# Twelve gate scatters and two gate loads moved across a block boundary in a decoder-layer kernel

## The reference, cut to what matters

```python
q = (tb @ wq).reshape(PEER_BLOCK, PEER_HEADS, 2, PEER_QHALF)
sc = jnp.einsum('thpd,hpnd->thpn', q, keys)
s1, i1 = lax.top_k(sc[:, :, 0], 16); s2, i2 = lax.top_k(sc[:, :, 1], 16)
# the best 16 of the 256 sums are the experts eidx, their softmax the gates g
act = jax.nn.gelu(jnp.einsum('td,thkd->thk', tb, u_tab[eidx]))
out = jnp.einsum('thk,thkd->td', g * act, v_tab[eidx])
```

## Time and profile before

| | us |
|---|---|
| median of three runs | 3581.18 (3580.72 to 3588.79) |
| the profiled execution | 3575.43 |
| its span, first to last instruction | 3573.7 |
| TensorE matmul busy | 3357.5 (94%) |
| VectorE busy | 2622.8 (73%) |
| GpSimd busy | 2051.8 (57%) |

### The profile page before, as it was taken

One profiled execution on the slowest core, in us unless ns is written; L12 is line 12 of the kernel. 1 busy time (PEld: TensorE's weight loads), 2 busy tenths in 40 slices (PEclk: granted clock), 3 DMA queues, 4 the chain that ended last, 5 costly groups with the idle time before them and its releaser, 6 DMA issues.

```text
span 3573.7 us, 41306 instructions
## 1 busy us (share of the span) xinstructions
PE 3357.5 (94%) x12551; PEld 1744.3 (49%) x12551; DVE 2622.8 (73%) x5429; ACT 842.2 (24%) x1786; POOL 2051.8 (57%) x1620
## 2 busy tenths in 40 slices
PE   8999799799899977799999999999999999999898
PEld 5676464444444445444444444444444444444343
DVE  3444584467778766578887888888888888888884
ACT  2333560344443465111111111111111111111021
POOL 0000100078888888577777777777777677777540
PEclk9999899899999988899999999999999999999999
DMA  4000631588889885899999999999999999999961
GB/s 148 30 29 15 243 146 68 179 213 213 205 211 233 226 229 147 263 396 407 405 407 398 400 406 404 403 394 406 406 406 404 396 391 407 405 401 398 355 218 42
DMA packets 410615, 1023.34 MB, mean 286 GB/s; under 512 B 93965, under 2 KB 130030, under 8 KB 406834
## 3 DMA queue, kind: packets, MB, share of 16 engines
q0 software_dynamic: 221184, 604.27, 46.6%
q1 hardware_dynamic: 175138, 394.69, 31.5%
q10 hardware_dynamic: 14096, 22.02, 1.7%
HBM read 972.05 MB, written 48.77 MB: 286 GB/s over the span
## 4 chain that ended last, share of the span: by engine, by line
POOL 21%; DMA 19%; issue 9%; DVE 7%; PE 2%; ACT 0%; DVEq 0%; SPq 0%; ACTq 0%; POOLq 0%
DMA u<-in_peer_u,idx_all 19%; POOL v L2165 11%; POOL u L2157 10%; DVE u L2175 2%; DVE facc L2203 2%; PE e_b L2319 1%; PE e_b L2090 1%; DVE wq L2203 1%; DMA w_room<-x_scratch 1%; DVE k_room L2105 1%; PE e_b L2307 0%; DVE ln_st L1060 0%; DVE w_room L2389 0%; DVE w_room L1073 0%; DVE w_room L2360 0%
## 5 line engine op out<-in xcount | busy, mean ns | idle before, releaser
L2157 POOL DMA_INDIRECT u<-in_peer_u,idx_all x576 | 724.8, 1258 | 393.2 <-DVE act L2175 246.4
L2090 PE MATMUL e_b<-w_room,e_room 128*128 128x512 f32 x2048 | 908.1, 597 | 21.7 <-DVE k_room L2105 12.8
L2175 DVE CUSTOM_DVE_ANT_0 u<-u,xb 128x1024 f32<-128x1024 f32 x576 | 705.7, 1225 | 295.1 <-DMA u<-in_peer_u,idx_all 268.5
L2058 PE MATMUL e_b<-wq 128*128 128x512 f32 x2048 | 900.3, 592 | 0.0
L2165 POOL DMA_INDIRECT v<-in_peer_v,idx_all x576 | 690.5, 1199 | 214.1 <-issue 177.5
L1782 POOL DMA_INDIRECT gate_scratch<-e_room,slot_of x384 | 610.4, 1590 | 188.3 <-issue 120.9
L2090 PEld LDWEIGHTS e_b<-w_room,e_room 128*128 128x128 f32 x2048 | 390.9, 191 | 519.4 <-issue 491.8
L2058 PEld LDWEIGHTS e_b<-wq 128*128 128x128 f32 x2048 | 379.5, 190 | 429.0 <-issue 429.0
L2203 DVE SCALAR_TENSOR_TENSOR facc<-v,w,facc 128x1024 f32<-128x1024 f32 x317 | 406.5, 1282 | 1.4
L2203 DVE SCALAR_TENSOR_TENSOR wq<-v,w,wq 128x1024 f32<-128x1024 f32 x254 | 325.9, 1283 | 0.5
L2051 ACT ACTIVATE wq<-e_b 128x512 f32<-128x512 f32 x256 | 140.0, 594 | 722.3 <-PE e_b L2044 473.2
(11 more groups left out here) (387 smaller groups left out, 3543.4 us busy)
## 6 DMA issues: line engine op xcount, KB each, us to landing
wq<-in_peer_u SPq DMA_DIRECT2D x128, 512.0 KB
w_room<-in_peer_v SPq DMA_DIRECT2D x128, 512.0 KB, 22.6
w_room<-in_cache_v SPq DMA_DIRECT2D x144, 256.0 KB
w_room<-in_cache_k SPq DMA_DIRECT2D x128, 256.0 KB
gate_scratch<-zeros SPq DMA_DIRECT2D x24, 1024.0 KB, 27.0
wq<-gate_scratch SPq DMA_DIRECT2D x96, 256.0 KB
u<-in_cache_k SPq DMA_DIRECT2D x64, 256.0 KB
xb<-in_cache_k SPq DMA_DIRECT2D x64, 256.0 KB
```

Of the source, the lines that this page charges most:

```text
L2058: last = pe.matmul(AQ[c % 2][:, 0:DT], UT[c % 2][:, k, :], x1Td[:, k, :], start=(k == 0), stop=(k == KC - 1))
L2090: last = pe.matmul(OQ[i % 2][b][:], WT[n % 2][:, c, m * P:m * P + P], Vd[(4 * n + c) % NVD][:, b * 512:b * 512 + 512], start=(c == 0), sto ...
L2157: pool.indirect_dma_start(u[x % NU], None, a["peer_u"], bass.IndirectOffsetOnAxis(ap=idx_all[:, t, h, j:j + 1], axis=0)).then_inc(s_u[x % ...
L2175: dve.tensor_tensor_reduce(u[x % NU], u[x % NU], xb[t % 2][:], 1.0, 0.0, ALU.mult, ALU.add, act16[k % 2][:, j:j + 1]).then_inc(s["ufree"], 1)
```

## The change

`scatter_pool` of the last head h = 7 issues ranks j = 0 to 11 only. Its last four ranks (`LATE_J = 4`), 4 x 3 = 12 scatters, are issued in the dense block by GpSimd: two behind each of the first six gather positions. `load_g(0)` leaves the end of the first block. In the dense block SP issues `load_g(0)` and `load_g(1)` behind `slot_sp(2)`, that is behind `load_u(5)`; the call for group 1 at x = 1 is gone.

```diff
-    LAG, WEIGH = 7, 5
+    LAG, WEIGH, LATE_J = 7, 5, 4
...
-        def scatter_pool(pool, h):
+        def scatter_pool(pool, h, js):
...
-            for j in range(TOPK):
+            for j in js:
                 for m in range(NSC):
                     if j == 0:
                         wait(pool, s_gs[m], 16 * TOPK * h)
-                    pool.indirect_dma_start(gate_d[m].rearrange("e (t o) -> (e t) o", o=1),
-                                            bass.IndirectOffsetOnAxis(ap=slot_of[:, m, h, j:j + 1], axis=0),
-                                            gd[:, m, h, j:j + 1], None, compute_op=ALU.add).then_inc(s_gs[m], 16)
+                    scatter_one(pool, h, j, m)
+
+        def scatter_one(pool, h, j, m):
+            pool.indirect_dma_start(gate_d[m].rearrange("e (t o) -> (e t) o", o=1),
+                                    bass.IndirectOffsetOnAxis(ap=slot_of[:, m, h, j:j + 1], axis=0),
+                                    gd[:, m, h, j:j + 1], None, compute_op=ALU.add).then_inc(s_gs[m], 16)
...
-            if x % 4 == 1 and x // 4 + 1 < NGR:
+            if x % 4 == 1 and 1 < x // 4 + 1 < NGR:
                 load_g(sp, x // 4 + 1)
...
                 load_x(sp, 1)
-                load_g(sp, 0)
...
-                    scatter_pool(pool, h)
+                    scatter_pool(pool, h, range(TOPK - (LATE_J if h == PH - 1 else 0)))
...
                     slot_sp(sp, x)
+                    if x == 2:
+                        load_g(sp, 0)
+                        load_g(sp, 1)
...
+                late = [(j, m) for j in range(TOPK - LATE_J, TOPK) for m in range(NSC)]
                 for x in range(NPOS + 12 + LAG):
                     gather_pool(pool, x)
+                    for j, m in late[2 * x:2 * x + 2]:
+                        scatter_one(pool, PH - 1, j, m)
```

## The result

The changed kernel takes 3592.53 us (median of 20 runs, 3582.47 to 3598.01), the kernel before in the same runs 3580.55 (3575.47 to 3590.75): ratio 1.0032, 95% interval 1.0024 to 1.0039. That is 12.0 us slower by the medians, where 11.4 was forecast (3592.6). The profiled execution took 3587.21 us, its span is 3585.4, against 3575.43 and 3573.7.

The account below looks back on a forecast made before the run. The barrier, then VectorE up to weigh(0, 0), then TensorE were taken to bound the kernel. VectorE 21.25 us later in the block, less 9.84 gained, gave +11.41 on the 3581.18 median: 3592.6 us, range 3584 to 3601.

Parts of the forecast that it names:

- The gain at the barrier: Barrier ahead of the dense block: without the last 12 scatters and `load_g(0)` the block starts 9.84 us earlier.
- T: The dense block's start, forecast at 1451.46: SP's last issue over at 1449.39, plus 2.07; 1461.30 before.
- GpSimd's string: Dense block: six gathers and 12 late scatters on GpSimd, the last scatter ready 31.5 us in (30.2 to 38.4).
- The landing of a scatter: Dense block: from the last late scatter being ready to SP going on, 5.45 us (2.4 to 6.3).
- rival A: Late scatters in the dense block land faster; at 2.4 us the net is +8.4, 3589.5 us; chance 0.23.
- The landing of the gate load: Dense block: the last of group 0's four 256 KB gate loads lands in 3.9 us, upper bound 10.3.
- Does it reach TensorE: From gating chunk 0 to weigh(0, 0): VectorE's delay reaches TensorE, weigh(0, 0) starts at 1527.6, 11.4 us later.
- rival C of the experiments: Ahead of the dense block: the changed programs are by themselves a few us slower there; no chance given.
- C: Gating of chunk 0: the wait stays hidden and the 9.84 us gain stands, 3571.3 us; chance 0.04.
- D: Barrier: something else holds it and the block starts no earlier, +21.3, 3602.4 us; chance 0.03.
- Rival E: Dense block: VectorE's 1.70 us and later idle times shrink, giving part back; net +8 to +9.5; chance 0.07.
- B: Crowded dense-block stretch: scatters at 2.22 or a gate load at 10.3, about +18, 3599 us; chance 0.11.

Follow-up runs that it names:

- second profile of before: Kernel before, unchanged, profiled once more, with TensorE's last scores group ahead of the barrier starting at 1455.54; ratio 1.0000 (0.9990 to 1.0009).

## Why the prediction was right in its sum, and where it wasn't in its terms

**What bounds the kernel.** Right. From weigh(0, 0) to the end both kernels need the same, 2057.5 and 2056.8.

**The gain at the barrier: mis-sized.** Forecast T = 1451.46, measured 1454.06 and 1459.90. The 9.84 us were read from one execution, in which TensorE was early and stood for 12.91 us. The profiles of before show that this idle time is a cover: TensorE's path ahead of it varies by 8 us, and the block's start by 1. The step of the argument that failed is "TensorE's own work ends at 1448.39", taken as a fixed date. At a like E the gain is 11.4 in an early execution (E to T 14.0 against 2.6) and about 4 in a late one (6.8 against 2.9). The 2.07 from SP's last issue to the block's start was carried over wrongly as well: where SP's issue holds the barrier it is 0.45, in the changed kernel (1453.61 to 1454.06) and in the late profiles of before. A sign was there: the profiled execution lay 5.75 below the median of the runs, which the prediction added back without asking what it was.

**GpSimd's string.** 31.5 forecast, 33.4 and 32.5 in the two profiles of the changed kernel (1487.42 - 1454.06; 1492.37 - 1459.90). Single scatters took 2.10 and 2.29, in the second profile 2.59, where the others took 1.54 to 1.57, and single gathers up to 1.92 where most took 0.99. By the Trainium skill (SBUF — State Buffer, section SBUF: two separate sides) the prediction had estimated that hold-ups beside five dot products could come to 6 us; the traces show 2 to 3.

**The landing of a scatter: mis-sized.** 5.45 forecast, 1.5 (1487.42 to 1488.91) and 1.7 measured for the last scatter: rival A, and even below its bound of 2.4. Both rows that the 5.45 was argued from stood in crowded stretches. The prediction held against A that the 6.29 was measured at a share of 0.63, but this is the mean of 123 us; in the 6.3 us of the landing itself the share was 1.08 (first line; the second is the landing ahead of the barrier, the third the one in the changed kernel; the last three numbers are clock, DMA share, GB/s):

```profile
1351.80:1358.10 6.30, 1.63 (x2) 0.35 (x3) 4.10 (x21) 0.00 (x0) 3.10 (x3) 0.56 1.08 342
1453.40:1458.90 5.50, 0.00 (x0) 0.00 (x0) 0.00 (x0) 0.00 (x0) 0.05 (x1) 0.50 1.11 380
1487.40:1488.90 1.50, 1.30 (x4) 0.23 (x2) 0.00 (x0) 0.00 (x0) 1.02 (x2) 1.00 0.26 0
```

So the reading that was held against A was a mean over the wrong stretch. The rule of the Trainium skill (DMA: Bandwidth & Descriptors, section Anatomy of one DMA), about 2 us for a transfer so small, was nearer than my row for this landing; at a share of 1.1 both landings took over twice as long as the rule says.

**The landing of the gate load.** 3.9 forecast, 4.4 (1488.91 to 1493.28) and 4.6 measured. The 2.6 that the prediction worked out for it goes by a rule that it gives itself as one for GpSimd's transfers; this load is SP's.

**The gating of chunk 0.** T + 40.85 forecast, T + 39.22 and T + 38.72 measured: 1.6 to 2.1 too late, since the scatter's landing outweighs the other two.

**Does it reach TensorE.** Right at every step. Gating 0 to weigh(0, 0) took 35.30 and 35.45, forecast 35.30. TensorE's stall ahead of it was 12.58, between the 5.4 and 16 that were named; meet 5 was over at T + 61.9, ahead of the latest date of T + 70.7. Weigh(0, 0) took 9.88 instead of 8.91, about 1 more, within the bounds of 0 and 1.9; but the second profile of before has 10.02 behind a stall of 6.72, so this isn't the change's.

**The sum.** In the first pair of profiles the net is 1528.58 - 1516.20 = 12.4 us at weigh(0, 0) and 11.7 at the end. That this is near the forecast is chance: 4.2 of the 12.4 is E, which happened to be later. At a like E the profiles say (the changed kernel's 77.1 is taken to hold at any E, as it does in its two profiles, at 1451.5 and 1457.0):

| | gain at the barrier | cost behind it | net |
|---|---|---|---|
| forecast | 9.84 | 21.25 | 11.4 |
| early (first profiles) | 11.4 | 19.6 | 8.2 |
| late (second profiles) | 3.9 | 17.8 | 13.9 |

For an execution like the one it was read from, the forecast set the gain 1.6 too low and the cost 1.6 too high, and the net came out 3.2 too high. For a late one it set the gain 6 and the cost 3.5 too high. The timed 12.0 (8.6 to 14.0) lies between the two nets, and so does the forecast: its closeness is luck.

The late case is the usual one by an estimate. The median of before in the same runs, 3580.55, less the 1.7 around the span and the 2056.2 to 2057.8 that its profiles have from weigh(0, 0) to the end, puts weigh(0, 0) at 1521.0 to 1522.6, where its three profiles have 1516.2 to 1518.7; with the 63.2 to 63.6 of the late profiles E is at 1457 to 1459. The same for the changed kernel (3592.53, 2056.7 and 77.1) gives 1457. By this estimate E is no later in the changed program, which speaks against rival C of the experiments, and the net to expect is nearer 13.9 than 8.2. It also fits that moving only the loads gained nothing: in late profiles E to weigh(0, 0) is 63.2 without that move and 63.2 with it. The estimate takes it that the end part is as long in the executions that weren't profiled; in the fourteen that were it is 2055.2 to 2059.4.

**The rivals.** Rivals C and D are out: the wait at the gating is there, and E to T fell. Rival E is out as well: from the gating of chunk 0 to weigh(0, 0) nothing was given back (35.30 and 35.45 against 35.30). A was right about the landing. Its net of +8.4 is what the early profiles have, and it didn't show in the timed runs, since in most executions the gain is smaller. B's price for a crowded stretch was paid elsewhere: with only the loads moved the gate loads took 11.3 us to land. That is not at the end of the changed kernel's string, where B looked for it, but in the first 25 us of the block, which I hadn't examined: the early block runs into the nine loads that used to move while TensorE stood at the barrier.

## What to carry to other kernels

An idle time ahead of a barrier that one profile shows can be the cover for a path that varies from run to run: before a change is credited with it, see in a second profile whether the late engine or the idle one moves. Work shifted behind a barrier lands on the same in-order engines that must make the block's first results; if the first consumer needs both the shifted work and the engine's own, dealing them in another order may change nothing, as it did here. A mean share over a long stretch doesn't tell how busy the DMA engines were in the few microseconds of one landing: take the window of the landing. And idle time at a barrier is also the time in which the next block's first loads travel: taking it away puts them in competition with the block's own.

## What the runs showed of the hardware that I had not expected

A scatter of 128 floats with an add landed 1.5 us after it was made at a DMA share of 0.26 (changed kernel) and 1.7 at 0.57 (its second profile), but 5.4 and 6.3 us after it at 1.11 and 1.08 (kernel before). A 256 KB load took 4.4 and 4.6 us at the end of the changed kernel's string and 11.3 at a share of 1.04 (only the loads moved). An issue on SP's queue that waits for nothing isn't of one length either: three in a row for 256 KB each took 1.45 us with only the loads moved, 3.62 ahead of the barrier in before with the twelve left out, and 9.25 for group 1 with the v loads behind group 0, one of them 4.04 alone; why is open.
